# Retrieval gates scattered into a DRAM table by adding indirect DMAs, instead of built by one-hot matmuls

## The chip, the cores and the metric

One core of a Trainium2 chip runs the whole program. The metric is device time in microseconds (us), of which three runs of the kernel before are given. TensorE is called PE in the profile (its weight load PEld), VectorE DVE, ScalarE ACT, GpSimd POOL, SyncE SP.

## The reference, cut to what matters

A layer with attention, a gated delta rule and a product-key retrieval of experts ("peer"), followed by a second layer that the change doesn't touch. There are 256 tokens of width 1024, all in float32. The retrieval, in blocks of 128 tokens:

```python
s1, s2 = scores of each of 8 heads against 128 + 128 sub-keys
v1, i1 = lax.top_k(s1, 16); v2, i2 = lax.top_k(s2, 16)
cand_s = v1[..., :, None] + v2[..., None, :]          # 256 candidates a head
cand_i = i1[..., :, None] * 128 + i2[..., None, :]
top_s, pos = lax.top_k(cand_s, 16)
experts = take_along_axis(cand_i, pos); gates = softmax(top_s)
act = gelu(einsum("thkd,td->thk", expert_down[experts], h))
out = einsum("thk,thkd->td", gates * act, expert_up[experts])
```

Each token thus uses 8 x 16 = 128 of the 128 x 128 experts, and an expert that two heads pick gets the sum of their gates.

## The kernel before

The retrieval is computed densely. All 16384 x 256 activations are computed ("down"), multiplied by a gate that is zero for an expert that isn't picked, and multiplied with all of `expert_up` ("up"). Weights stream from DRAM through a ring of four 1 MB slots (`Stream`, loads issued by SP at L94). Each slot is four units of 128 x 512. Every unit is split in a high part (ACT, `split_hi`, L285) and the rest (DVE, `split_lo`, L290), for three float32r products on PE. There are four buffers for the parts, so ACT splits unit u once PE is done with unit u - 4, and DVE and PE follow.

Down is 256 units in 32 groups of 8, each unit 12 matmuls (L1833). After each group, ACT applies Gelu to the group's 128 x 1024 results (`gelu(c)`, L1876), into a staging tile, and issues a store of it to `act_spill` in DRAM (L1880). Up is 256 units as well, each 6 matmuls of 512 columns (L300). For each 8 units of it, ACT loads 512 KB of activations back (`load_acts`, L1886), DVE multiplies them by the gates (`weights`, L2017), ACT and DVE split the products (L1893, L2022), and PE waits for the split.

The gates are made beside down. DVE does the `routing` between its splits: the top 16 of each score row, the candidates, their top 16, and the look-up of the two sub-key indices by comparing and summing (L1940 to L1998), which must be done six units before group 20 (`GATE0`). ACT takes one exponential (L1908), DVE normalizes, PE transposes the picks (six transposes). Then, in 64 of the units from group 20 on, DVE makes for 4 tokens a one-hot of the first index (L2007) and a gated one-hot of the second (L2010), PE multiplies them (L1819) to a 128 x 128 gate matrix for each token, and ACT copies it into the gates' place in SBUF (L1897). PE, ACT and DVE run this order as it is written; nothing is planned at run time.

Ahead of it stands the delta rule's stage (blocks at L1230 and L1321), in which POOL's first instruction is a small memset (L1241) and ACT's are two exponentials (L1249, L1250) and then two larger ones that wait for DVE (L1252, L1253). SP loads tiles of `w_ada` there (`load_fills`, L441), which PE and DVE sum as filler work (L460, L449), seven tiles deep. POOL's only DMAs in the kernel before are two in the first stage (L702, L706) and the gate row's store and load near the end of up (L479, L484).

Of the kernel before, what the change touches and what calls it, by code (L numbers as in the profile page):

```python
# [16 lines left out]
F32 = mybir.dt.float32  # L17
# [126 lines left out]
def build(nc, A, out):  # L144
    with ExitStack() as ctx:
# [7 lines left out]
        act_spill = nc.dram_tensor("act_spill", (P, P * S), F32, kind="Internal").ap()  # L153
# [1072 lines left out]
        qgT = at(O_X_HI + 512, HD, P)  # L1226
        (s_zero, s_gbias, s_gexp, s_diff, s_dexp, s_beg, s_tk, s_kk, s_L, s_dv) = (sem("dn_" + n) for n in (
            "inverse_cleared", "gate_bias_loaded", "gate_exps", "differences", "decays", "beta_decay",
            "k_transposed", "grams", "lower", "steps"))
        with nc.Block() as block:  # L1230
# [417 lines left out]
        with nc.Block() as block:  # L1648
# [5 lines left out]
            def _(sp):  # L1654
# [5 lines left out]
                sp.wait_ge(s_sp, 16)  # L1660

# [100 lines left out]
        GT = 4  # L1762
        NB4 = S // GT
        GATE0 = 20
        slots = [8 * c + u for c in range(GATE0, 31) for u in (1, 2, 3, 5, 6, 7)][:NB4]
        slot_of = {u: b for b, u in enumerate(slots)}
        one1 = [at(O_ONE + i * GT * P, GT, P) for i in range(2)]
        one2 = [at(O_ONE + 1024 + i * GT * P, GT, P) for i in range(2)]
        staged = at(O_ST, 1024)
        G = at(O_R, P, S)  # L1770
        pick = lambda i, t, n=1: at(O_PICKS + i * S + t, n)
        (s_G, s_st, s_route, s_dv, s_e, s_gn, s_t, s_pt, s_o1, s_o2, s_gm, s_ge) = (sem("experts_" + n) for n in (
            "gelu", "acts_stored", "routed", "steps", "exp", "normed", "picks_transposed", "picksT", "onehot1",
            "onehot2", "gate_product", "gate_out"))
# [16 lines left out]
        with nc.Block() as block:  # L1791
            @block.gpsimd
            def _(pool):
                nc.clear_and_free_semaphores(query_sems)
                store_gate(pool)
                load_gate(pool, gate2)
# [14 lines left out]
            def _(pe):  # L1811
                def gates(b):

                    pe.wait_ge(s_o1, b + 1)
                    pe.wait_ge(s_o2, b + 1)
                    if b >= 4:
                        pe.wait_ge(s_ge, b - 3)
                    for j in range(GT):
                        mm = pe.matmul(ps[:, 4 + b % 4, j * P:(j + 1) * P], one1[b % 2][:, j, :], one2[b % 2][:, j, :],  # L1819
                                       start=True, stop=True)  # L1820
                    mm.then_inc(s_gm, 1)

                for c in range(DG):
                    if c >= 2:
                        pe.wait_ge(s_G, c - 1)
                    for k in range(KT):
# [10 lines left out]
                        if u == KT * GATE0 - 2:  # L1837
                            pe.wait_ge(s_gn, 1)
                            transposes(pe, [(psf[:, 2048 + (i * TT + tt) * P:2048 + (i * TT + tt + 1) * P],
                                             pickT[:, i, tt * P:(tt + 1) * P])  # L1840
                                            for i in range(3) for tt in range(TT)]).then_inc(s_t, 1)
                        if u in slot_of:
                            gates(slot_of[u])
# [9 lines left out]
                pe.wait_ge(s_ge, NB4)  # L1853
# [17 lines left out]
            def _(act):  # L1871
                def gelu(c):
                    act.wait_ge(unit_used, used_value(g0 + KT * c + 7))
                    if c:
                        act.wait_ge(s_st, 16 * c)
                    act.activation(staged, psf[:, c % 2 * 1024:(c % 2 + 1) * 1024], ACT.Gelu).then_inc(s_G, 1)  # L1876

                def store(c):
                    act.wait_ge(s_G, c + 1)
                    act.dma_start(act_spill[:, c * 1024:(c + 1) * 1024], staged).then_inc(s_st, 16)  # L1880

                def load_acts(q):
# [3 lines left out]
                    act.dma_start(got[q % 2], act_spill[:, q * 1024:(q + 1) * 1024]).then_inc(s_rd[q % 2], 16)  # L1886
# [8 lines left out]
                def gate_out(b):  # L1895
                    act.wait_ge(s_gm, b + 1)
                    act.copy(G[:, :, b * GT:(b + 1) * GT],  # L1897
                             ps[:, 4 + b % 4, :].rearrange("p (t i) -> p i t", i=P)).then_inc(s_ge, 1)

                for u in range(KT * DG):  # L1900
# [3 lines left out]
                    if u % 8 == 4 and u > 8:  # L1904
                        store(u // 8 - 1)
                    if u == KT * GATE0 - 5:
                        act.wait_ge(s_route, 1)
                        act.activation(pickT[:, 2, :], pickT[:, 2, :], ACT.Exp).then_inc(s_e, 1)  # L1908
                    if u - 5 in slot_of:
                        gate_out(slot_of[u - 5])  # L1910
# [7 lines left out]
                store(DG - 1)  # L1918
                for i in range(3, 2 * P):
                    split_hi(act, n1 + i // UPC, g1 + i, i % UPC, 0)  # L1920
                    q = i // 8
                    if i == 3:
                        act.wait_ge(s_st, 16 * DG)
                        load_acts(1)
                    if i % 8 == (3 if q else 6) and q + 1 < UG:
                        weights_hi(q + 1)
                    if i % 8 == 7 and q + 2 < UG:
                        load_acts(q + 2)
# [4 lines left out]
            def _(dve):  # L1933
# [26 lines left out]
                def routing():  # L1960

                    yield from top16(score, best, best_at, range(TT * 2 * NH))
                    step(dve.tensor_copy(best_ix, u32(best_at)))
                    yield
                    for tt in range(TT):
                        for hd in range(NH):
                            a = best[:, tt * 16 + 2 * hd, :]
                            b = best[:, tt * 16 + 2 * hd + 1, :]
                            one = dve.tensor_tensor(cand[:, tt * NH + hd, :].rearrange("p (a b) -> p a b", b=TOP), wide(a, TOP),
                                                    b.unsqueeze(1).to_broadcast([P, TOP, TOP]), ALU.add)  # L1970
                            yield
                    step(one)
                    yield from top16(cand, picked, picked_at, range(TT * NH))
                    for tt in range(TT):
                        at_ = u32(at(O_V + 1792 + tt * P, P))

                        step(dve.tensor_scalar(u32(part_u[:, 0, :]), at_, 4, None, ALU.logical_shift_right))
                        step(dve.tensor_scalar(u32(part_u[:, 1, :]), at_, 15, None, ALU.bitwise_and))
                        step(dve.tensor_copy(part_of, u32(part_u)))
                        yield  # L1980
                        eq = at(O_M, P, TOP)
                        for half in range(2):
                            step(dve.tensor_tensor(eq, wide(part_of[:, half, :], TOP),
# [960 lines left out]
```

## Time and profile before

| | |
|---|---|
| three runs, median (lowest to highest) | 1671.28 us (1668.65 to 1673.79) |
| profiled execution, span from first to last instruction | 1673.4 us |
| PE, DVE, ACT, POOL busy, share of the span | 95%, 73%, 54%, 2% |
| DMA moved | 313.85 MB, mean 188 GB/s, in the best of 40 slices 364 GB/s |
| mean granted TensorE clock | 0.979 of full speed |

The profiled execution's own time is its span and what lies around it; the span is 2.1 us above the median of the runs and 0.4 us below the slowest, so that span and run time are taken as one here, with an offset of 2.1 us. In the rows, the busy us of a group are the union of its instructions; matmuls overlap, so that the mean ns of one says nothing of their pace, while their count over a stretch does.

### The profile page before, as it was taken

How to read it: one execution, taken by the hardware profiler on the slowest of the kernel's cores; microseconds unless marked ns; L12 is line 12 of the kernel's file. 1: busy time of each engine (PE TensorE's matmuls, PEld its weight loads, DVE VectorE, ACT ScalarE, POOL GpSimd, SP SyncE). 2: the span in 40 equal slices, each digit the busy share in tenths (PEclk: the TensorE clock that was granted, in tenths of full speed). 3: DMA queues.
4: the chain of work that ended last, by engine and by line, in shares of the span. 5: the costliest groups of instructions: out<-in, count | busy, mean ns of one | idle time of the engine just before them, and what ended most of it. 6: DMA issues, size and time to landing. Idle time of an engine off the chain costs nothing. (4 is left out here: it accounts for less than half of the span.)

```text
span 1673.4 us, 26490 instructions
## 1 busy us (share of the span) xinstructions
PE 1587.1 (95%) x10351; PEld 1426.7 (85%) x10351; DVE 1224.7 (73%) x2475; ACT 906.1 (54%) x1518; POOL 41.7 (2%) x82
## 2 busy tenths in 40 slices
PE   5998888999999999999999999899999898989998
PEld 5877767999999999988888888797888677789997
DVE  5876765889997999867667777657886666654664
ACT  6775455554545555555555555546556646455453
POOL 0023000000000000000000000110000000000000
PEclk9999899999999999999999999999999899999999
DMA  9944343667766555567788767554443122445552
GB/s 327 364 161 128 102 159 125 213 217 235 229 205 213 158 158 151 165 229 248 237 293 289 250 234 245 202 177 151 151 150 128 63 89 101 151 151 177 181 197 101
DMA packets 111665, 313.85 MB, mean 188 GB/s; under 512 B 9441, under 2 KB 10041, under 8 KB 102073
## 3 DMA queue, kind: packets, MB, share of 16 engines
q1 hardware_dynamic: 100008, 276.95, 49.9%
q10 hardware_dynamic: 11040, 33.66, 5.9%
q8 instruction: 82, 1.34, 0.3%
q0 software_dynamic: 496, 1.59, 0.3%
q14 instruction: 39, 0.31, 0.1%
HBM read 293.28 MB, written 18.89 MB: 187 GB/s over the span
## 5 line engine op out<-in xcount | busy, mean ns | idle before, releaser
L300 PE MATMUL ps<-parts,parts 128*128 128x512 f32 (+1 forms) x4992 | 972.4, 357 | 20.1 <-DVE parts L290 18.1
L300 PEld LDWEIGHTS ps<-parts,parts 128*128 128x128 f32 x4992 | 824.3, 191 | 155.9 <-DVE parts L290 19.1
L285 ACT CAST parts<-lead 128x512 fp32r<-128x512 f32 x940 | 579.1, 620 | 619.9 <-PE ps L300 394.1
L290 DVE TENSOR_TENSOR parts<-lead,parts 128x512 fp32r<-128x512 f32 x940 | 641.1, 688 | 328.8 <-ACT parts L285 324.8
L1833 PE MATMUL ps<-parts,parts 128*128 128x256 f32 x3072 | 385.3, 285 | 4.5 <-DVE parts L290 4.5
L1833 PEld LDWEIGHTS ps<-parts,parts 128*128 128x128 f32 x3072 | 372.6, 192 | 5.6 <-DVE parts L290 5.6
L376 PE MATMUL ps<-lead,mem 128*128 128x128 f32 (+2 forms) x292 | 46.5, 323 | 41.0 <-ACT mem L520 23.2
L376 PEld LDWEIGHTS ps<-lead,mem 128*128 128x128 f32 (+2 forms) x292 | 40.9, 162 | 47.5 <-ACT mem L520 24.6
L2010 DVE TENSOR_SCALAR mem<-lead,mem 128x128 f32<-128x128 f32 x256 | 71.1, 341 | 0.0
L1819 PE MATMUL ps<-mem 128*128 128x128 f32 x512 | 67.9, 275 | 0.7 <-DVE mem L2010 0.7
L1819 PEld LDWEIGHTS ps<-mem 128*128 128x128 f32 x512 | 62.8, 192 | 1.2 <-issue 1.1
L2007 DVE TENSOR_SCALAR mem<-lead,mem 128x128 f32<-128x128 f32 x256 | 55.5, 280 | 0.0
L2017 DVE TENSOR_TENSOR mem<-mem 128x1024 f32<-128x1024 f32 x32 | 39.1, 1221 | 7.5 <-DMA mem<-act_spill 7.3
L2022 DVE TENSOR_TENSOR parts<-mem,parts 128x1024 fp32r<-128x1024 f32 x32 | 39.0, 1219 | 0.5 <-ACT parts L1893 0.5
L1897 ACT COPY mem<-ps 128x512 f32<-128x512 f32 x64 | 37.0, 579 | 0.0
L1893 ACT CAST parts<-mem 128x1024 fp32r<-128x1024 f32 x32 | 33.5, 1047 | 5.7 <-DVE mem L2017 5.7
L1876 ACT ACTIVATE mem<-ps 128x1024 f32<-128x1024 f32 x32 | 32.7, 1020 | 0.8 <-PE ps L1833 0.8
L2198 PEld LDWEIGHTS ps<-mem 128*128 128x128 f32 x256 | 29.8, 192 | 0.6
L2198 PE MATMUL ps<-mem 128*128 128x128 f32 x256 | 29.9, 275 | 0.0
L1348 PEld LDWEIGHTS ps<-mem 64*64 64x64 f32 x512 | 18.2, 151 | 6.3 <-POOL mem L1333 4.0
L1348 PE MATMUL ps<-mem 64*64 64x64 f32 x512 | 19.5, 238 | 4.3 <-POOL mem L1333 2.5
L479 POOL DMA_DIRECT2D gate_rows<-mem x1 | 0.6, 577 | 885.9 <-DVE mem L2066 885.9
(348 smaller groups left out, 994.3 us busy)
## 6 DMA issues: line engine op xcount, KB each, us to landing
lead<-in_peer_expert_down SPq DMA_DIRECT2D x64, 1024.0 KB, 5.5
lead<-in_peer_expert_up SPq DMA_DIRECT2D x64, 1024.0 KB, 5.8
lead<-in_w_in SPq DMA_DIRECT2D x50, 1024.0 KB, 5.2
lead<-in_w_ffn_in SPq DMA_DIRECT2D x22, 1024.0 KB, 5.2
act_spill<-mem ACTq DMA_DIRECT2D x32, 512.0 KB, 5.1
mem<-act_spill ACTq DMA_DIRECT2D x32, 512.0 KB, 3.6
mem<-in_w_ada SPq DMA_DIRECT2D x29, 512.0 KB, 6.9
lead<-in_w_ffn_out SPq DMA_DIRECT2D x11, 1024.0 KB, 4.9
```

Source lines behind the costliest of these rows:

```text
L285: act.copy(w_hi[g % BUFFERS], st.words(n, u * UNIT, UNIT)).then_inc(hi_ready, 1)
L290: dve.tensor_tensor(w_lo[g % BUFFERS], st.words(n, u * UNIT, UNIT), w_hi[g % BUFFERS].bitcast(F32), ALU.subtract).then_inc(lo_ready, 1)
L300: mm = pe.matmul(o, lhs[a], rhs[b], start=start and i == 0, stop=stop and i == 2, skip_group_check=True, **kw)
L376: last = pe.transpose(o, i, ident[0:i.shape[0], 0:i.shape[0]])
L1348: mm = pe.matmul(ps[rows, bank, u % 4 * HP:(u % 4 + 1) * HP], left[rows, :], right[rows, :], start=True, stop=True)
L1819: mm = pe.matmul(ps[:, 4 + b % 4, j * P:(j + 1) * P], one1[b % 2][:, j, :], one2[b % 2][:, j, :], start=True, stop=True)
L1833: mm = pe.matmul(ps[:, c % 2 * 2 + m // 2, m % 2 * S:(m % 2 + 1) * S], parts[a][:, ms], (x_hi, x_lo)[b][:, k, :], start=k == 0 and i == 0 ...
L2007: one = dve.tensor_scalar(one1[b % 2][:, j, :], iota, pick(0, b * GT + j), None, ALU.is_equal)
L2010: one = dve.tensor_scalar(one2[b % 2][:, j, :], iota, pick(1, b * GT + j), pick(2, b * GT + j), ALU.is_equal, ALU.mult)
L2017: dve.tensor_tensor(got[q % 2], got[q % 2], at(O_R + q * 1024, 1024), ALU.mult).then_inc(s_pr, 1)
L2022: dve.tensor_tensor(a_lo[q], got[q % 2], a_hi[q].bitcast(F32), ALU.subtract).then_inc(s_al, 1)
L2198: mm = pe.matmul(psf[:, 2048 + u * P:2048 + (u + 1) * P], k, q, start=True, stop=True)
```

## The change

The activations stay in SBUF, in the place that the gates had, and nothing of them goes to DRAM. In their stead a table of the gates, `gate_table` (16 MB, cell = 32768 x first index + 256 x second index + token), lies in DRAM. It is cleared in the delta rule's stage: POOL zeroes a 128 x 1024 tile ahead of its other work, and ACT, once that is done and ahead of its exponentials, issues four DMAs of 4 MB that repeat the tile. SP waits for them at the end of the query stage.

The routing is cut in 8 groups, one for each pair of heads and half of the tokens, each spread over 24 units of down; each ends with the cells' numbers and the exponents in SBUF. ACT takes each group's exponential at the 24th unit, and DVE normalizes it in three steps in the next group's units 1 to 3. POOL then issues 256 indirect DMAs, each of which adds 128 gates (one a token) to 128 cells of the table. They go in batches of 16, by head and, within a head, by token half; a batch waits for its group's gates, and for the batch of the head before of the same token half to have landed, since two heads may pick one cell. Four units ahead of the end of down ACT waits for all 256, and then issues the loads of the table, 512 KB for each 8 units of up. The one-hots, their products, their copies, the transposes and the stores are gone.

```diff
+                pool.memset(blank, 0.0).then_inc(s_blank, 1)
+                pool.wait_ge(s_blank, 1)
                 pool.memset(TI_all[HP:P, :, 0:HP], 0.0).then_inc(s_zero, 1)
...
             def _(act):
+                act.wait_ge(s_blank, 1)
+                for i in range(4):
+                    act.dma_start(gate_table[:, i * 8192:(i + 1) * 8192].rearrange("p (a b) -> p a b", b=1024),
+                                  blank.unsqueeze(1).to_broadcast([P, 8, 1024])).then_inc(s_cleared, 16)
                 act.activation(eg_, gc_, ACT.Exp).then_inc(s_gexp, 1)
...
                 sp.wait_ge(s_sp, 16)
+                sp.wait_ge(s_cleared, 64)
...
+        GU = 24
+        read_by = {20: 1, 21: 5, 22: 7, 23: 7, 24: 8}
+        cells = bass.AP(gate_table.tensor, 0, [[1, P * P * S], [1, 1]])
...
+                for hd in range(NH):
+                    for tt in range(TT):
+                        pool.wait_ge(s_gn, TT * (hd // 2) + tt + 1)
+                        if hd:
+                            pool.wait_ge(s_put[tt], 16 * TOP * hd)
+                        for j in range(TOP):
+                            c = (tt * NH + hd) * TOP + j
+                            pool.indirect_dma_start(
+                                out=cells, out_offset=bass.IndirectOffsetOnAxis(ap=picks[0][:, c:c + 1].bitcast(U32), axis=0),
+                                in_=picks[1][:, c:c + 1], in_offset=None, compute_op=ALU.add).then_inc(s_put[tt], 16)
                 store_gate(pool)
...
-                        if u in slot_of:
-                            gates(slot_of[u])
...
                 def gelu(c):
                     act.wait_ge(unit_used, used_value(g0 + KT * c + 7))
-                    if c:
-                        act.wait_ge(s_st, 16 * c)
-                    act.activation(staged, psf[:, c % 2 * 1024:(c % 2 + 1) * 1024], ACT.Gelu).then_inc(s_G, 1)
+                    if c in read_by:
+                        act.wait_ge(s_route, read_by[c])
+                    act.activation(acts[:, c * 1024:(c + 1) * 1024], psf[:, c % 2 * 1024:(c % 2 + 1) * 1024], ACT.Gelu)\
+                        .then_inc(s_G, 1)
...
+                    if u % GU == GU - 1 and u // GU < GROUPS_R:
+                        r = u // GU
+                        act.wait_ge(s_route, r + 1)
+                        v = picks[1][:, gate_cols(r)]
+                        act.activation(v, v, ACT.Exp).then_inc(s_e, 1)
                     if u == KT * DG - 5:
-                        act.wait_ge(s_gm, NB4)
-                        load_acts(0)
+                        for tt in range(TT):
+                            act.wait_ge(s_put[tt], 16 * TOP * NH)
+                        load_gates(0)
...
                     if i == 3:
-                        act.wait_ge(s_st, 16 * DG)
-                        load_acts(1)
+                        load_gates(1)
...
+                    one = dve.scalar_tensor_tensor(out=full_ix, in0=pair[:, :, 0, :], scalar=float(P * S), in1=low_ix,
+                                                   op0=ALU.mult, op1=ALU.add)
...
                     dve.wait_ge(s_rd[q % 2], 16 * (q // 2 + 1))
+                    dve.wait_ge(s_G, q + 1)
```

## Rows read from the trace of the kernel before

**Rows 1.** The page: busy us, share of the span and instructions of each engine.
```profile
PE 1587.1 (95%) x10351; PEld 1426.7 (85%) x10351; DVE 1224.7 (73%) x2475; ACT 906.1 (54%) x1518; POOL 41.7 (2%) x82
```

**Rows 2.** Table of stretches of down: length, busy us (count), PEclk, DMA share, GB/s.
```profile
292.70:507.00 214.30, 212.11 (x1759) 211.29 (x1760) 199.52 (x596) 108.29 (x167) 0.00 (x0) 1.00 0.68 221
530.00:711.00 181.00, 180.25 (x1537) 179.94 (x1537) 168.47 (x592) 93.17 (x161) 0.00 (x0) 1.00 0.52 161
```

**Rows 3.** The timeline: start us, us, what; begin and end of down.
```profile
292.68 7.58 PE L1833 MATMUL ps<-parts,parts 128*128 128x256 f32 x61 [2.35 <-DVE parts L290]
...
709.05 14.64 PE L1833 MATMUL ps<-parts,parts 128*128 128x256 f32 x120
723.52 8.72 PE L300 MATMUL ps<-parts,parts 128*128 128x512 f32 x36
```

**Rows 4.** Table of one stretch ahead of the gates, L1833 alone: PE, PEld busy.
```profile
331.20:474.50 143.30, 142.70 (x1190) 142.50 (x1189) 1.00 0.71 231
```

**Rows 5.** The page, costliest groups: busy us, mean ns; idle before.
```profile
L1819 PE MATMUL ps<-mem 128*128 128x128 f32 x512 | 67.9, 275 | 0.7 <-DVE mem L2010 0.7
...
L1876 ACT ACTIVATE mem<-ps 128x1024 f32<-128x1024 f32 x32 | 32.7, 1020 | 0.8 <-PE ps L1833 0.8
```

**Rows 6.** DVE's groups of instructions from 292.7 to 507.0 us, the costliest.
```profile
L290 DVE TENSOR_TENSOR parts<-lead,parts 128x512 fp32r<-128x512 f32 x147 | 100.0, 686 | 14.2 <-ACT parts L285 13.2
```

**Rows 7.** The timeline around the one change of ACT's table in down.
```profile
504.80 20.32 PE L1833 MATMUL ps<-parts,parts 128*128 128x256 f32 x168
...
516.64 1.28 ACT L1908 ACT_TABLE_LOAD   x1
...
517.93 0.42 ACT L1908 ACTIVATE mem<-mem 128x256 f32<-128x256 f32 x1
```

**Rows 8.** The timeline from the end of down into up, ACT and DVE.
```profile
712.29 0.33 ACTq L1886 DMA_DIRECT2D mem<-act_spill  x1
...
725.14 0.62 ACT L285 CAST parts<-lead 128x512 fp32r<-128x512 f32 x1 [0.40 <-PE ps L300]
...
727.40 0.33 ACTq L1886 DMA_DIRECT2D mem<-act_spill  x1
...
732.63 1.22 DVE L2017 TENSOR_TENSOR mem<-mem 128x1024 f32<-128x1024 f32 x1 [2.86 <-DMA mem<-act_spill]
...
734.52 13.69 PE L300 MATMUL ps<-parts,parts 128*128 128x512 f32 x52 [2.27 <-DVE parts L290]
```

**Rows 9.** The timeline of the delta rule's stage, where the clearing goes.
```profile
138.93 0.52 POOL L1241 MEMSET mem<- 64x512 f32 x1 [18.89 <-POOLq L1014]
138.95 0.21 ACT L1249 ACTIVATE lead<-lead 128x8 f32<-128x8 f32 x1 [0.27 <-PEq L1014]
...
140.77 4.26 SPq L441 DMA_DIRECT2D mem<-in_w_ada  x3
...
141.75 1.06 ACT L1252 ACTIVATE mem<-mem 128x1024 f32<-128x1024 f32 x1 [2.08 <-DVE mem L1271]
...
153.29 2.08 DVE L449 SCALAR_TENSOR_TENSOR mem<-mem,lead 128x1024 f32<-128x1024 f32 x1
```

**Rows 10.** Lines L971 (POOL's largest memset) and L1880 (ACT's stores), ns min/median/max.
```profile
L971 POOL MEMSET mem<- x2: 737/1014/1292, 109.8 to 1081.3; 128x768 f32 x1, 128x896 f32 x1
...
L1880 ACTq DMA_DIRECT2D act_spill<-mem x32: 326/327/360, 307.5 to 724.8; - x32
...
DMA to landing us min/median/max: 2.6/5.1/8.7
```

**Rows 11.** POOL's DMAs in the timeline, and the landing of the gate row's two.
```profile
49.89 1.83 POOL L706 DMA_DIRECT2D mem<-rel_ext  x2 [6.39 <-DMA rel_ext<-mem]
...
1050.67 0.58 POOL L484 DMA_DIRECT2D lead<-gate_rows  x1 [2.97 <-DMA gate_rows<-mem]
...
DMA to landing us min/median/max: 3.2/5.6/8.0
```

**Rows 12.** A POOL instruction that reads SBUF beside a busy DVE, ns min/median/max.
```profile
L978 POOL TENSOR_SCALAR_AFFINE_SELECT mem<-mem x13: 238/537/966, 110.8 to 1091.3; 128x64 f32<-128x64 f32 x13
```

More of the change, by code:

```diff
@@ L1761, in build, with gate_cols @@
         query_sems = retired()
[L1762 to L1774, printed above, removed]
+        PAIRS = NH // 2
+        GROUPS_R = TT * PAIRS
+        GU = 24
+        picks = [at(O_PICKS, 2 * P), at(O_PICKS + 2 * P, 2 * P)]
+        token = at(O_PICKS + 4 * P, TT)
+        low_ix = at(O_PICKS + 4 * P + 64, 2, TOP)
+        full_ix = at(O_PICKS + 4 * P + 96, 2, TOP)
+        eq = at(O_ONE, 4 * TOP, TOP)
+        part_u = at(O_ONE + 1024, 4, TOP)
+        part_of = at(O_ONE + 1088, 4, TOP)
+        found = at(O_ONE + 1152, 4, TOP)
+        acts = at(O_R, P * S)
+        def gate_cols(r):
+            c = (r % TT * NH + r // TT * 2) * TOP
+            return slice(c, c + 2 * TOP)
+        read_by = {20: 1, 21: 5, 22: 7, 23: 7, 24: 8}
+        cells = bass.AP(gate_table.tensor, 0, [[1, P * P * S], [1, 1]])
+        (s_G, s_tok, s_route, s_dv, s_e, s_gn) = (sem("experts_" + n) for n in (
+            "gelu", "tokens", "routed", "steps", "exp", "gates"))
+        s_put = [sem(f"experts_scattered{tt}") for tt in range(TT)]
         n0, g0 = n_down
@@ L1811, in _ @@
             def _(pe):
[L1812 to L1821, printed above, removed]
                 for c in range(DG):
@@ L1836, in _ @@
                         mm.then_inc(unit_used, 1)
[L1837 to L1841, printed above, removed]
-                        if u in slot_of:
-                            gates(slot_of[u])
                 def half(i, tt):
@@ L1917, in _ @@
                 gelu(DG - 1)
-                store(DG - 1)
                 for i in range(3, 2 * P):
@@ new lines, in gates @@
+                def gates(r):
+                    dve.wait_ge(s_e, r + 1)
+                    v = picks[1][:, gate_cols(r)].rearrange("p (h j) -> p h j", j=TOP)
+                    total, inverse = tiny[:, 2 * r:2 * r + 2], tiny[:, 32 + 2 * r:34 + 2 * r]
+                    one = dve.tensor_reduce(total, v, AX, ALU.add)
+                    yield
+                    step(one)
+                    one = dve.reciprocal(inverse, total)
+                    yield
+                    step(one)
+                    dve.tensor_tensor(v, v, wide(inverse, TOP), ALU.mult).then_inc(s_gn, 1)
@@ L2022, in weights_lo @@
                     dve.tensor_tensor(a_lo[q], got[q % 2], a_hi[q].bitcast(F32), ALU.subtract).then_inc(s_al, 1)
-                route = routing()
                 for u in range(KT * DG):
                     if u == KT * DG - 1:
-                        dve.wait_ge(s_ge, NB4)
                         weights(0)
                     split_lo(dve, n0 + u // UPC, g0 + u, u % UPC, 0)
-                    for _ in range(3 if u % 4 == 3 else 2):
-                        next(route, None)
-                    if u == KT * GATE0 - 6:
-                        for _ in route:
-                            pass
-                    if u == KT * GATE0 - 3:
-                        dve.wait_ge(s_e, 1)
-                        g3 = pickT[:, 2, :].rearrange("p (a j) -> p a j", j=TOP)
-                        step(dve.tensor_reduce(tiny[:, 0:16], g3, AX, ALU.add))
-                        step(dve.reciprocal(tiny[:, 16:32], tiny[:, 0:16]))
-                        dve.tensor_tensor(g3, g3, wide(tiny[:, 16:32], TOP), ALU.mult).then_inc(s_gn, 1)
-                    if u == KT * GATE0 + 1:
-                        dve.wait_ge(s_t, 1)
-                        dve.tensor_copy(at(O_PICKS, 3 * S), psf[:, 2048:2048 + 3 * S]).then_inc(s_pt, 1)
-                        dve.wait_ge(s_pt, 1)
-                    if u - 2 in slot_of:
-                        gated_onehots(slot_of[u - 2])
+                    r, v = divmod(u, GU)
+                    if r < GROUPS_R:
+                        if v == 0:
+                            route = routing(r)
+                        for _ in range(3 if v % 2 else 2):
+                            next(route, None)
+                        if v == GU - 3:
+                            for _ in route:
+                                pass
+                    if 1 <= r <= GROUPS_R:
+                        if v == 1:
+                            gate = gates(r - 1)
+                        if 1 <= v <= 3:
+                            next(gate, None)
                 weights_lo(0)
```

117 lines of the change are left out of this document (53 added, 64 removed).

## The prediction

> **What bounds the kernel now.** I read the page first, then the waits, the table of stretches for down, and the timeline at each edge of the change. On the page [rows 1] PE is busy 95% of the span and POOL 2%: work taken off PE counts, and POOL has room. The stretches [rows 2] show down in two parts. Up to 507 us PE is busy 212.1 of 214.3 us with DVE at 199.5: PE sets the pace, DVE is close behind. From 530 to 711 us, with the gates' work, PE is busy 180.3 of 181.0 us. Down runs from 292.7 to 723.5 us [rows 3], 430.8 us, and PE hardly waits in it. The clock is the full one in all of it (granted 1.00, so 2.4 GHz), so a matmul that goes is time that goes, as long as no one else becomes late.
>
> **Part 1, PE's gate products go.** Without them down's matmuls go at 1190 in 143.3 us [rows 4], 0.1204 us each; the last 120 of down, when the gates are done, take 14.47 us [rows 3], 0.1206 each. Down has 256 units x 12 = 3072 of them: 3072 x 0.1204 = 369.9 us. Down gets shorter by 430.8 - 369.9 = 60.9 us. The gates' own row agrees roughly: 512 products, 67.9 us busy, overlapping with others [rows 5]. DVE's one-hots and ACT's copies go too, and they are worth nothing by themselves, since they lay beside PE.
>
> **Part 2, the routing in 8 groups.** DVE's routing is 199.5 - 100.0 = 99.5 us [rows 2, 6], 12.4 us a group. A group has 24 units, 24 x 1.445 = 34.7 us of PE, in which DVE also splits for 24 x 0.686 = 16.5 us: 28.9 of 34.7 us. In the 18 units where the group's steps really lie it is 12.4 + 12.3 of 26.0 us, 95%, as tight as before (93%), where PE lost 2.2 us in the stretch. More small steps wait for their predecessor now, but the four units of buffers smooth that. I take 0, between -2 (the loss goes) and +2.
>
> **Part 3, ACT's exponentials.** Eight instead of one, and each changes ACT's table there and back: 2 x 1.28 us [rows 7] and a short exponential. ACT has 24 x 0.62 + 3 x 1.02 = 17.9 us of work [rows 5, 8] per group of 34.7 us, so the 3 us fit; around the one change before, PE ran 20.3 us without a break [rows 7]. Cost 0, covered by the units that are split ahead; with no cover it would be 8 x 3 = 24 us. In the group of Gelu, an output in SBUF instead of in the staging tile costs the same, and the store's issue (0.33 us on ACT) goes.
>
> **Part 4, the edge into up.** The second load of activations was issued at 727.40 us, after a wait for the last store; DVE then sat 2.86 us for it and PE 2.27 us [rows 8]. The table's load has no store to wait for and can go when the split that starts at 725.14 is handed over, at 725.8: 1.6 us earlier. -1.6 us. The loads themselves are as large as before.
>
> **Part 5, the clearing.** POOL's 128 x 1024 memset is 1.47 us (896 columns take 1.29, [rows 10]), so that ACT may go at 140.4 instead of 138.95 us [rows 9]. It issues four DMAs at 0.33 us and some 0.1 between them [rows 10]: 142.1. Then its two exponentials: 142.9, and the larger one, which began at 141.75, begins 1.15 us late; DVE and the stage's end wait behind it. +1.2 us; bounds 0 and 3.2 (all of ACT's delay). The data, 16 MB are 46 us at the 364 GB/s of the profile's best slice and 73 us at the 231 of [rows 4], so they last from 141 to somewhere between 187 and 214 us. Beside them SP's tile loads: the first is issued at 140.77 and used at 153.29 [rows 9], 12.5 us later; 512 KB land in about 5 us [rows 10], and at half the rate, 10 us, are still there in time. DMA from ACT and from SP do share: ACT's 512 KB stores land in 2.6 us at best and 5.1 in the median beside SP's stream [rows 10], not after a queue of megabytes. The Trainium skill, "DMA: Bandwidth & Descriptors", section "Queues, rings and completion order", says that each engine takes turns among the queues packet by packet; the landings agree.
>
> **Sum, if POOL keeps up.** -60.9 + 0 + 0 - 1.6 + 1.2 = -61.3 us. The profiled span 1673.4 becomes 1612.1; the run's median lies 2.1 us under the span, so 1671.3 - 61.3 = **1610 us**.
>
> **Part 6, does POOL keep up?** This is the choice on which the sign hangs. Let d be the time from one indirect DMA to the next on POOL. ACT's wait stands where the first load is issued now, 11.2 us before the end of down (712.29 against 723.52, [rows 3, 8]): at 292.7 + 369.9 - 11.2 = 651.4 us. Behind it on ACT are the table's first load, then every split of the rest of down and of up; DVE and PE wait for those, so lateness goes into the time one for one. The last DMAs must also land: POOL's DMA that writes DRAM takes 3.2 us [rows 11], so POOL must be done at 648.2. Gates of group 1 are ready at about 292.7 + 2 x 34.7 + 2 = 364.1, and since head 0's first batch alone can go before that, 240 DMAs remain: d must be under 284.1 / 240 = 1.18 us. After group 7, at 572.3, 48 remain: 1.58 us, looser. Each batch waits for one whose last DMA was issued 16 d before, 14.7 us at d = 0.92, longer than the slowest landing of 8.0 [rows 11]: no cost.
>
> The trace has no indirect DMA. Rows near it: one plain DMA of 128 rows holds POOL for 0.58 us, and one of 128 x 8 short rows of 512 B for 0.92 (two in 1.83, [rows 11]). An address for each of 128 cells is nearer to the second: I take 0.92, hidden with 0.26 us to spare on each. A DMA whose offsets are read from SBUF may also be held up by DVE: the same small POOL instruction takes 0.24, 0.54 and 0.97 us (least, median, most, [rows 12]), 0.3 or 0.73 us more beside a busy DVE. That makes d 1.22 or 1.65. The far bound is one DMA at a time, 3.2 us: 240 x 2.02 = 485 us late.
>
> The Trainium skill has a rule against this change ("SBUF — State Buffer", "Who interferes with whom"): DVE instructions with two SBUF inputs lock POOL's reads out, and copies in a two-port mode its descriptor writing; the spread of rows 12 agrees with the first. Its section "A bandwidth-pool intuition that's wrong (but worth ruling out)" has a POOL DMA go from 0.62 to 3.1 us beside such copies. As an estimate from that page, d = 3.1 would be 240 x 1.92 = 461 us late; down's DVE work is splits, not such copies, so I give it no more than the tail of the third case.
>
> **The cases.**
> - Hidden (chance 0.52): d under 1.18 us, 1610 us, its own range 1604 to 1618 from the bounds of parts 2 and 5. For it: POOL is idle all through down, and the 0.92.
> - POOL late, gain left (0.18): d between 1.18 and 1.44, where 240 (d - 1.18) reaches 61.3. At 1.22 it is 10 us late, 1620 us; in the middle 1640.
> - POOL late, slower than before (0.19): d over 1.44. At 1.65, the largest hold-up of rows 12, 240 x 0.47 = 113 us late: 1723 us. This is the case on the other side; it decides at 1.44 us per DMA, half as much again as the 0.92.
> - The cells choke the DMA engines (0.05). The weights, 67.1 MB in 369.9 us, are 181 GB/s; at 0.52 of the engines for 161 GB/s [rows 2] that is 0.59. What is left, 0.41 x 369.9 x 16 engines over 32768 cells, is 74 ns for each read, addition and write. No row prices one. A 4 KB packet (a store of 8 to an engine lands in 2.6 us, [rows 10]) takes 325 ns at most; at 150 ns a cell the engines would need 218 + 307 us: 155 us over, 1765 us.
> - The clearing holds SP's tiles up (0.06): if they go behind all 16 MB, the one due at 153.3 lands at 187: +34, 1644, if not later us. Against it: the stores' landings.
>
> **Numbers.** A change of 0.3% (5 us) is about what a measurement of this kernel can tell from none. Faster by more: 0.52 + 0.17 of the second case + 0.06 = 0.75. Within: 0.02. Slower: 0.23. The range reaches down to 1604 and up over the two middle cases to the third at d = 1.65, 1725 us; left out are the third beyond it (about 0.09) and most of the fourth. It is wide because cases of both signs carry weight; the likeliest one's own is 1604 to 1618.
>
> **What the profile after would show.** Part 1: L1833's 3072 matmuls in 370 us, and no PE work between them. Part 2: DVE under 90% in down's first 192 units and PE with no idle. Part 3: 16 or so table loads, no PE wait at them. Part 6: the distance between POOL's DMAs, and the end of the last against ACT's first load of the table; if ACT waits there for POOL or the scatter's landing, PE has one long gap just before up. Part 5: ACT's larger exponential 1.2 us later, no DVE or PE wait for a `w_ada` tile. What would make the prediction wrong, first of all, is a d over 1.2 us; next a stream load in down that lands late.

## The result, and the profile after

The changed kernel takes 1845.24 us (1843.36 to 1850.15), the kernel before, on the same chip, 1672.53 (1668.65 to 1674.69): a ratio of 1.104, 95% interval 1.1018 to 1.1062. That is 172.7 us slower, where 61 us faster was forecast. The page of the profile after, against [rows 1], says where to look:

```profile
span 1843.4 us, 25145 instructions
PE 1527.2 (83%) x9833; PEld 1369.1 (74%) x9833; DVE 1116.8 (61%) x2022; ACT 892.6 (48%) x1475; POOL 462.8 (25%) x340
...
PE   6994788999999980000699999998999988989999
...
POOL 1013000178788777878200000002000000000000
PEclk9996899999999995555799999999999989999999
DMA  9939453577777762222577887774444322345553
```

PE has 59.9 us less to do than before, as intended, and a hole of four slices near the middle. POOL is at work up to the end of the hole. A smaller dip stands in the fourth slice, where the table is cleared. The timeline of PE, ACT and POOL around the hole (start us, us):

```profile
653.81 31.12 PE L1853 MATMUL ps<-parts,parts 128*128 128x256 f32 x258
893.92 7.79 PE L1853 MATMUL ps<-parts,parts 128*128 128x256 f32 x48 [208.99 <-DVE parts L290]
...
892.08 0.34 ACTq L1895 DMA_DIRECT2D mem<-gate_table  x1
892.52 2.18 ACT L285 CAST parts<-lead 128x512 fp32r<-128x512 f32 x4 [211.77 <-DMA gate_table<-mem]
...
885.53 1.55 POOL L1823 DMA_INDIRECT gate_table<-mem  x1 [0.30 <-issue]
889.05 1.54 POOL L1823 DMA_INDIRECT gate_table<-mem  x1 [1.97 <-issue]
```

PE names DVE, DVE waited for ACT, and ACT for the cells. ACT's wait is the one ahead of the table's first load; it lasts until the 256th indirect DMA, which leaves POOL at 890.59, has landed, and the load is issued at 892.08, 1.5 us behind it. So the kernel waits for POOL. POOL's group, and its timeline near the first of the pauses ("issue" marks idle time that nothing in the profile ends):

```profile
L1823 POOL DMA_INDIRECT gate_table<-mem x256 | 419.6, 1639 | 150.2 <-issue 111.2 <-DVE mem L2023 39.0
...
359.76 1.72 POOL L1823 DMA_INDIRECT gate_table<-mem  x1 [38.98 <-DVE mem L2023]
...
386.11 1.55 POOL L1823 DMA_INDIRECT gate_table<-mem  x1 [0.30 <-issue]
387.96 1.55 POOL L1823 DMA_INDIRECT gate_table<-mem  x1 [0.30 <-issue]
393.44 1.54 POOL L1823 DMA_INDIRECT gate_table<-mem  x1 [3.92 <-issue]
```

An adding DMA holds POOL for 1.55 us, the next begins 0.30 us later, and the 16th, the 32nd and so on wait 1.8 to 4.1 us. The 151 that are issued while DVE works take up to 2.38 us, 1.70 in the mean; the 105 in the hole take at most 1.57. Over all the mean is 1.64. From 359.76 to 890.59 us it is 2.07 us for each of 256: this is the d of the prediction, which took 0.92 and had 1.18 as the limit of what is hidden.

The second loss stands in the delta rule's stage, against [rows 9]:

```profile
139.00 0.95 POOL L1243 MEMSET mem<- 128x1024 f32 x1 [18.92 <-POOLq L1014]
...
139.99 24.72 ACTq L1255 DMA_DIRECT2D gate_table<-mem  x4
164.75 0.21 ACT L1257 ACTIVATE lead<-lead 128x8 f32<-128x8 f32 x1 [26.00 <-issue]
...
140.97 16.82 SPq L441 DMA_DIRECT2D mem<-in_w_ada  x3
...
173.70 1.97 PE L1356 MATMUL ps<-mem 64*64 64x64 f32 x32 [25.53 <-POOL mem L1341]
```

ACT is held for 24.7 us by the issue of four DMAs. It is not the single issue that costs, as narrower stretches of ACT's timeline show, up to 140.6 us and from 152 us:

```profile
139.99 1.02 ACTq L1255 DMA_DIRECT2D gate_table<-mem  x2
...
151.80 12.91 ACTq L1255 DMA_DIRECT2D gate_table<-mem  x1
```

Two DMAs go out in 1.0 us, the third takes 10.7 us and the fourth 12.9. So everything that waits for ACT's exponentials is late: POOL's mask, its products, and PE by 25.5 us. SP's issue of three tiles takes 16.8 us where it took 4.3. The table of stretches (length, busy us of PE, PEld, DVE, ACT, POOL, PEclk, DMA share, GB/s) closes the account:

```profile
321.80:684.93 363.13, 363.13 (x3024) 362.92 (x3024) 276.59 (x763) 204.04 (x306) 256.86 (x151) 1.00 0.72 183
684.93:893.92 208.99, 0.00 (x0) 0.00 (x1) 0.75 (x2) 1.40 (x3) 162.73 (x105) 0.51 0.22 1
893.92:1250.00 356.08, 356.08 (x1585) 295.70 (x1585) 256.60 (x343) 190.09 (x293) 1.19 (x2) 0.99 0.75 254
```

Down begins at 321.8 us and not at 292.7 [rows 3]: +29.1. Its work takes 3024 matmuls in 363.1 us at the full clock, without a gap, and 48 more behind the hole: 370.7 us without the hole, 60.1 less than 430.8. The hole is +209.0. Up, from its first matmul to the transposes that follow it (901.55 to 1256.43, before 723.52 to 1082.64), takes 354.9 us and not 359.1: -4.2. The sum is 29.1 - 60.1 + 209.0 - 4.2 = +173.8; the spans differ by 170.0, and the 3.8 us between them lie behind up, where they were not followed. In the hole the granted clock is 0.51, the lower level of 1.2 GHz; behind it PE works at 0.99 in the stretch, so the hole costs little beyond its length.

### The profile page after: what moved, and what is told of

It reads as the page before. It is cut to its first block and busy times, and to the rows that moved or that the text cites. A ratio compares the mean times of both kernels' runs of the same rounds, so it can differ in the third digit from the quotient of the medians.

```text
span 1843.4 us, 25145 instructions
## 1 busy us (share of the span) xinstructions
PE 1527.2 (83%) x9833; PEld 1369.1 (74%) x9833; DVE 1116.8 (61%) x2022; ACT 892.6 (48%) x1475; POOL 462.8 (25%) x340
## 5 line engine op out<-in xcount | busy, mean ns | idle before, releaser
L1853 PE MATMUL ps<-parts,parts 128*128 128x256 f32 x3072 | 370.9, 284 | 211.3 <-DVE parts L290 211.3
L1823 POOL DMA_INDIRECT gate_table<-mem x256 | 419.6, 1639 | 150.2 <-issue 111.2
L1356 PE MATMUL ps<-mem 64*64 64x64 f32 x512 | 21.5, 251 | 31.2 <-POOL mem L1341 25.5
L2205 PEld LDWEIGHTS ps<-mem 128*128 128x128 f32 x256 | 29.8, 192 | 0.6
L2205 PE MATMUL ps<-mem 128*128 128x128 f32 x256 | 29.9, 275 | 0.0
L971 POOL MEMSET mem<- 128x768 f32 (+1 forms) x2 | 2.0, 1025 | 75.8 <-PE ps L376 45.7
L787 DVE SCALAR_TENSOR_TENSOR lead<-lead 128x1024 f32<-128x1024 f32 x16 | 18.9, 1218 | 1.1 <-DMA lead<-in_w_ada 1.1
L2701 ACT ACTIVATE mem<-mem 128x2048 f32<-128x2048 f32 x8 | 15.3, 1916 | 5.8 <-DVE mem L2414 5.8
```

The lines of the kernel that those rows point to most:

```text
L1356: mm = pe.matmul(ps[rows, bank, u % 4 * HP:(u % 4 + 1) * HP], left[rows, :], right[rows, :], start=True, stop=True)
L1823: pool.indirect_dma_start(out=cells, out_offset=bass.IndirectOffsetOnAxis(ap=picks[0][:, c:c + 1].bitcast(U32), axis=0), in_=picks[1][:, c ...
L1853: mm = pe.matmul(ps[:, c % 2 * 2 + m // 2, m % 2 * S:(m % 2 + 1) * S], parts[a][:, ms], (x_hi, x_lo)[b][:, k, :], start=k == 0 and i == 0 ...
L2205: mm = pe.matmul(psf[:, 2048 + u * P:2048 + (u + 1) * P], k, q, start=True, stop=True)
```

## Experiments

Two theories are told apart. **POOL's pitch**: the hole is 256 DMAs at 2.07 us, and the rest of the change does what was forecast. **The cells' traffic**: additions to single cells in DRAM slow the weights' stream or land late, whatever POOL does. Beside them stands the clearing, with its own question: what of it costs the 29 us. "Before" was run beside them four times over: medians of 1671.07 to 1673.64 us.

**no_scatter.** POOL's loop over the batches is taken out, so that every gate is zero, and ACT waits for the gates and not for the cells.

```diff
-                        for tt in range(TT):
-                            act.wait_ge(s_put[tt], 16 * TOP * NH)
+                        act.wait_ge(s_gn, GROUPS_R)
```

> The changed kernel with all 256 indirect DMAs left out, so that every gate is zero; all else, the clearing too, is as changed. Theory: the one long wait of 212 us behind the scatter is the whole of the loss in the expert stage. Then the time is 1845 - 212 = 1633 us (1628 to 1640), and down takes 370 us. Rival: the table's loads or the activations in SBUF cost something of their own, then it stays above 1650.

Measured: 1633.84 us, ratio 0.9776 (0.9759 to 0.9793). Without the DMAs the same kernel is faster than before, and of the 211.4 us that separate it from the changed one the hole is 209.0.

**pool_clear, both_out, clear_2k.** Three ways to find what the clearing costs. In the first POOL issues the four DMAs, behind its last product of the stage; the second is that without the scatter; the third leaves them with ACT but cuts their rows from 4 KB to 2.

```diff
-                act.wait_ge(s_blank, 1)
-                for i in range(4):
-                    act.dma_start(gate_table[:, i * 8192:(i + 1) * 8192].rearrange("p (a b) -> p a b", b=1024),
-                                  blank.unsqueeze(1).to_broadcast([P, 8, 1024])).then_inc(s_cleared, 16)
...
                 one.then_inc(s_gz, 1)
+                for i in range(4):
+                    pool.dma_start(gate_table[:, i * 8192:(i + 1) * 8192].rearrange("p (a b) -> p a b", b=1024),
+                                   blank.unsqueeze(1).to_broadcast([P, 8, 1024])).then_inc(s_cleared, 16)
```

and in clear_2k:

```diff
-                    act.dma_start(gate_table[:, i * 8192:(i + 1) * 8192].rearrange("p (a b) -> p a b", b=1024),
-                                  blank.unsqueeze(1).to_broadcast([P, 8, 1024])).then_inc(s_cleared, 16)
+                    act.dma_start(gate_table[:, i * 8192:(i + 1) * 8192].rearrange("p (a b) -> p a b", b=512),
+                                  blank[:, 0:512].unsqueeze(1).to_broadcast([P, 16, 512])).then_inc(s_cleared, 16)
```

> The whole scatter; the four clearing DMAs are issued by POOL, behind its last work in the delta rule's stage, instead of by ACT. Theory: ACT was held for 25 us while it issued them, and the data themselves cost nothing: 1845 - 27 = 1818 us (1814 to 1822). Rival: the 16 MB on the DMA engines delay the tiles and weights wherever they run: 1830 us or more.

> No scatter (all gates zero) and the clearing on POOL. Theory: both losses are gone and what is left is the sum of the prediction, 1607 to 1613 us. Rival: some of the PE time that was taken out doesn't come back: 1620 us or more.

> The changed kernel with the clearing in rows of 2 KB instead of 4 KB: the same bytes from ACT, twice as many rows. Theory of rows: ACT is held until a fixed number of rows is left to be moved, so the hold grows from 25 us towards the time of the data, to 33 us or more. Theory of bytes: the hold stays at 25 us.

Measured: pool_clear 1837.91 us (ratio 1.101, 1.0981 to 1.1038), both_out 1630.59 (0.9758, 0.9741 to 0.9776), clear_2k 1855.61 in one run. The first two missed by 20 us, so both of their rivals had the number. POOL's timeline in pool_clear, then ACT's in clear_2k, show why:

```profile
160.77 2.69 POOL L1346 DMA_DIRECT2D gate_table<-mem  x3
201.98 0.88 POOL L1346 DMA_DIRECT2D gate_table<-mem  x1 [38.53 <-issue]
```

```profile
139.88 40.57 ACTq L1255 DMA_DIRECT2D gate_table<-mem  x4
180.50 0.21 ACT L1257 ACTIVATE lead<-lead 128x8 f32<-128x8 f32 x1 [41.86 <-issue]
```

Three DMAs of 1024 rows go out on POOL in 2.7 us, and the fourth is held for 38.5. The stage ends only when all engines have, so the stage waited: PE sits 20.1 us at its end, 2.4 before. It goes on at 214.65 us, 11.8 after the fourth issue; what fills these was not followed. With twice the rows ACT is held for 40.6 us in place of 24.7, though its first DMA, of 2048 rows, still goes out in 0.39 us. So the rows that are under way count, as if only so many could be outstanding, and not the bytes, which are the same; the limit itself was not measured. That the engine which issues is held was the part of the theory that stood; that POOL in ACT's place would not be held, as the forecast of 1818 supposed, was wrong.

**split_clear, split_clear_no_scatter.** Three of the clearing DMAs on POOL in the delta rule's stage, the fourth in the query stage, where POOL has nothing else to do (the diff is against pool_clear); then that without the scatter. All kernels from here on are built on split_clear.

```diff
                 one.then_inc(s_gz, 1)
-                for i in range(4):
+                for i in range(0, 3):
...
                 nc.clear_and_free_semaphores(first_sems)
+                for i in range(3, 4):
+                    pool.dma_start(gate_table[:, i * 8192:(i + 1) * 8192].rearrange("p (a b) -> p a b", b=1024),
+                                   blank.unsqueeze(1).to_broadcast([P, 8, 1024])).then_inc(s_cleared, 16)
```

> The whole scatter; POOL issues three of the clearing DMAs behind its work in the delta rule's stage and the fourth in the query stage. In the version with all four in the first place POOL was held 38.5 us ahead of the fourth, and the stage's end waited 20 us for POOL. Theory: that hold was all that the clearing cost, the 16 MB beside the weights cost nothing: 1838 - 20 = 1818 us (1812 to 1822). Rival: the data themselves delay the weights, 1830 us or more.

> As before it, with no indirect DMA (all gates zero). Theory: what is left is the prediction's sum, 1672.5 - 61 = 1611 us (1606 to 1615). Rival: 1620 us or more, then something beside the scatter and the clearing's hold costs time.

Measured: 1827.81 us (1.094, 1.0906 to 1.0973) and 1617.97 (0.9674, 0.9646 to 0.9703). Both lie 7 to 10 us above what was expected. PE's timeline in split_clear has the rest of the price:

```profile
170.32 1.98 PE L1355 MATMUL ps<-mem 64*64 64x64 f32 x33 [4.24 <-issue]
...
201.81 3.65 PE L376 MATMUL ps<-lead,mem 128*128 128x128 f32 x16 [7.80 <-PEq L1325]
```

Two waits, 4.2 us inside the stage (1.0 before) and 7.8 at its end (2.4 before), make down begin at 303 us, 10 us later than before. SP's issue of weight tiles is slow meanwhile (three in 11.0 us from 167.44 on); that the waits come from there was not tried by itself.

**half_scatter, three_quarters_scatter.** Heads 0 to 3, and 0 to 5: 128 and 192 DMAs.

```diff
-                for hd in range(NH):
+                for hd in range(4):
...
-                            act.wait_ge(s_put[tt], 16 * TOP * NH)
+                            act.wait_ge(s_put[tt], 16 * TOP * 4)
```

> The split clearing, and only heads 0 to 3 scattered: 128 indirect DMAs (half of the gates left out). At the 2.07 us that one took on average they end 332 + 265 = 597 us into the span, before ACT's wait at 651. Theory: the scatter costs only by being late, so the time is that of the version with none, 1611 us (within 4). Rival: the cells' additions slow the weight stream, or POOL's work slows DVE, by some 20 us or more.

> The split clearing, and heads 0 to 5 scattered: 192 indirect DMAs (a quarter of the gates left out). Theory of lateness one for one: the end is at 332 + 192 x 2.07 + 3 = 732 us, 81 us behind the 651 of ACT's wait: 1611 + 81 = 1692 us (1684 to 1698). Rival: the lateness is taken up in part by work that goes on, 1675 us or less.

Measured: 1615.1 us (0.9659, 0.9631 to 0.9687) and 1704.61 (1.0198, 1.0169 to 1.0228). PE's timeline in half_scatter at the edge into up, and in three_quarters_scatter:

```profile
671.76 258.59 PE L300 MATMUL ps<-parts,parts 128*128 128x512 f32 x1140
```

```profile
749.63 7.26 PE L1855 MATMUL ps<-parts,parts 128*128 128x256 f32 x48 [84.07 <-DVE parts L290]
```

```profile
744.70 1.55 POOL L1825 DMA_INDIRECT gate_table<-mem  x1 [1.90 <-issue]
```

This separates the theories. 128 DMAs, 16384 cells, cost nothing: the time is that without any (1617.97), down takes 368.7 us, and PE has no gap at all into up. Were the traffic the cost, half of it would show. The trace after has the cells' price: their queue, from 360 to 680 us of down,

```profile
q0 software_dynamic: 21265, 0.09, 14.0%
```

has 21265 packets in 14.0% of the time of 16 engines, 34 ns for each. From 192 on each DMA adds (1827.81 - 1704.61) / 64 = 1.93 us, POOL's pitch in the time when DVE stands still (1.55 + 0.30 + 1.9 / 16 = 1.97). Three quarters came out 12 us over the expectation. The gap is 84.1 us where 81 was expected; most of the rest is the base, 1617.97 and not 1611. (The last DMA ended at 746.3 us and not near 729, but ACT's wait, too, began some 10 us later.)

**plain_cells, cells_of_64, extra_waits, plain_cells_of_64.** What the pitch is made of: without the addition, with half of the cells to a DMA, with three more waits (already satisfied) in each batch, and the first two together. The edits of the first three, in this order:

```diff
-                                in_=picks[1][:, c:c + 1], in_offset=None, compute_op=ALU.add).then_inc(s_put[tt], 16)
+                                in_=picks[1][:, c:c + 1], in_offset=None).then_inc(s_put[tt], 16)
...
-                                out=cells, out_offset=bass.IndirectOffsetOnAxis(ap=picks[0][:, c:c + 1].bitcast(U32), axis=0),
-                                in_=picks[1][:, c:c + 1], in_offset=None, compute_op=ALU.add).then_inc(s_put[tt], 16)
+                                out=cells, out_offset=bass.IndirectOffsetOnAxis(ap=picks[0][0:64, c:c + 1].bitcast(U32), axis=0),
+                                in_=picks[1][0:64, c:c + 1], in_offset=None, compute_op=ALU.add).then_inc(s_put[tt], 16)
...
+                            if j and j % 4 == 0:
+                                pool.wait_ge(s_gn, TT * (hd // 2) + tt + 1)
```

> split_clear with the 256 indirect DMAs writing their cells instead of adding them (gates of experts that two heads picked are lost). Theory: GpSimd's 1.55 us is the making of 128 descriptors' worth of work and does not depend on the add: 1.55 us each, time 1828 +- 4. Rival: the add is what costs, a plain cell costs what the plain DMA of L706 did, 0.92 us: the last is issued near 341 + 256 x 1.3 = 674 and the time falls to about 1618.

> split_clear with each of the 256 indirect DMAs carrying the cells of 64 tokens instead of 128 (half the gates are left out). Theory: most of the 1.55 us is paid for each cell: about 0.8 to 1.0 us each, pitch about 1.3 us, time 1620 to 1640. Rival: it is paid for each DMA: 1.4 us or more each, time 1800 or more, and only fewer DMAs would help.

> split_clear with a wait that is already satisfied ahead of every fourth indirect DMA of a batch (three more in each batch of 16). It tells what the pause of 1.9 to 4.1 us in each batch is. Theory A: it is GpSimd's own, once in 16 DMAs, and stands before the 16th, the 32nd and so on, not where the waits are: the pauses stay at 16 in number, pitch 2.07 us, time 1828 +- 5. Theory B: a wait costs it: some 48 x 4 = 192 more waits (three in each of 16 batches are 48) give 48 more pauses of 2.5 us, about +120 us, 1945.

> plain_cells with the cells of 64 tokens to a DMA (half the gates are left out). From 128 to 64 cells an adding DMA fell from 1.55 to 1.42 us; without the add one of 128 took 0.97 us. Theory (a fixed part of each DMA makes most of it, cells cost about 2 ns each and the add about 0.55 us for each DMA, not for each cell): 0.84 to 0.91 us each, GpSimd's last near 666, time 1618 to 1632. Rival (the add costs by the cell, or plain DMAs cost by the cell): well under 0.8 us and 1618, or 0.97 as before and 1665.

Measured, in one run each: 1669.77, 1770.46, 1833.32 and 1656.73 us. POOL's line in the four kernels, in that order (ns least/median/most, first and last start us):

```profile
L1825 POOL DMA_INDIRECT gate_table<-mem x256: 965/992/2038, 342.8 to 714.4; - x128
```

```profile
L1825 POOL DMA_INDIRECT gate_table<-mem x256: 1419/1423/2336, 340.5 to 810.0; - x128
```

```profile
L1827 POOL DMA_INDIRECT gate_table<-mem x256: 1549/1555/2383, 343.0 to 872.6; - x128
```

```profile
L1825 POOL DMA_INDIRECT gate_table<-mem x256: 897/903/1516, 343.6 to 696.9; - x128
```

From the least of each: a plain DMA of 64 cells takes 0.90 us and one of 128 0.97, 1.1 ns a cell; adding ones 1.42 and 1.55, 2.0 ns a cell. The addition costs 0.52 to 0.58 us for each DMA, and the cells little: if each costs the same, 128 of them make 0.14 of the 0.97 us and 0.26 of the 1.55, and the rest is paid once for each DMA. Half the cells save 57 us in all, by the groups' rows 30 us in the DMAs (mean 1.639 to 1.523 us) and 34 in the idle time between them (111.5 to 77.4), since the pauses are gone, less 3.6 us of wait for the second group's gates. For plain_cells neither theory had the time: its durations were the rival's (0.97, not 1.55), but the last DMA was issued at 714.4 us and not near 674. With a mean of 1.115 us and the gap of 0.30 the pitch is 1.42 and not the 1.3 taken, 30 us, and the wait for the second group's gates is 9.8. PE's gap is 50.5 us. plain_cells_of_64 had the expected duration and came 25 us over, with a mean of 1.008 us, a wait of 13.9 us for the second group's gates, and three short pauses; PE's gap there is 32.0 us.

extra_waits settles half of the pauses' question. POOL's timeline in it:

```profile
371.28 1.55 POOL L1827 DMA_INDIRECT gate_table<-mem  x1 [0.30 <-issue]
376.92 1.55 POOL L1827 DMA_INDIRECT gate_table<-mem  x1 [4.08 <-issue]
```

It is the 16th again, 16 pauses as before, and none at the added waits: the pause is not a wait's. In plain_cells and in cells_of_64 there is none, only waits for DVE's gates, but plain_cells_of_64 has three, of 1.3 to 2.3 us, before its 52nd, 100th and 148th. The two kernels below, whose DMAs are adding ones of 128 cells too, have twelve of 1.8 to 6.2 us, before the 16th, 29th, 31st, 46th and so on. So the step of 16 is no fixed rule, and what causes the pauses stays open.

**half_by_products, half_by_products_rows.** Since 128 DMAs are hidden, token half 0 gets its gates by them and half 1 by the one-hot products of before. The table has half the columns and is cleared by two DMAs, and the activations of half 1 go through DRAM. The second kernel lays a loaded tile out as two blocks of 512 words, so that its rows are 2 KB and not 512 B. The one-hot products are 32 blocks of four tokens, in units 201 to 242. The core of it:

```diff
-                hp, tt = divmod(r, TT)
+                tt, hp = divmod(r, PAIRS)
...
+                    act.activation(acts[:, 4 * c:4 * c + 4, 0:P], pre[:, :, 0:P], ACT.Gelu)
+                    act.activation(staged, pre[:, :, P:S], ACT.Gelu).then_inc(s_G, 1)
...
+                        if u in slot_of:
+                            gates(slot_of[u])
...
-                    act.dma_start(got[q % 2], gate_table[:, q * 1024:(q + 1) * 1024]).then_inc(s_rd[q % 2], 16)
+                    for src, n in ((gate_table, 0), (act_spill, 512)):
+                        act.dma_start(got[q % 2][:, n:n + 512], src[:, q * 512:(q + 1) * 512]).then_inc(s_rd[q % 2], 16)
```

> Tokens 0 to 127 get their gates by the adding indirect DMAs (128 of them), tokens 128 to 255 by one-hot products as in the kernel before (32 blocks of four tokens, three transposes); the table has 128 columns a row group and is cleared by two DMAs on GpSimd in the delta rule stage; the activations of tokens 128 to 255 go through DRAM. The result is the reference's. Theory (GpSimd's pitch of 2.07 us is what makes the change slow, and half the DMAs are hidden): down takes 368.7 us as in half_scatter plus 32 blocks at (430.8 - 368.7) / 64 = 0.97 us, 399.7 us; 1615.1 + 31.0 = 1646, less up to 10 us because half the clearing is gone: 1641, between 1634 and 1649, faster than both kernels. Rival 1: each batch of 16 now waits for its own predecessor's landing, 15 us seven times, so the last lands near 727 and ACT waits some 27 us: about 1668. Rival 2: what the change gave came only with all the products gone (VectorE or ScalarE becomes the bound of down with both kinds of work): 1672 or more.

> half_by_products with the tiles got laid out as two blocks of 512 words, tokens 0 to 127 and tokens 128 to 255, so that each of the two loads writes rows of 2 KB and not of 512 bytes (VectorE's product and TensorE's slices follow the layout). The result is the reference's. In half_by_products up's VectorE waited 35.3 us for the loads of act_spill and TensorE 14.8 us behind it. Theory (the short rows made the loads land late): these 14.8 us go, 1659.7 - 15 = 1645, between 1640 and 1650. Rival (two DMAs in place of one, whatever their rows, or ScalarE's second issue): 1655 to 1660.

Measured: 1659.69 us (0.9928, 0.9908 to 0.9947) and 1651.98 (0.9884, 0.9846 to 0.9922). Both compute the whole of the reference and beat both kernels, by 0.7% and 1.2% against before. Down came out as expected, 295.2 to 693.9 us, 398.7 against 399.7. POOL did wait for landings, as the first rival had it, but six times 2.3 to 5.6 us and not seven times 15; its last DMA ended at 663.6 us, ahead of ACT's first load at 682.8, so nothing waited for it. The miss of 19 us lies in up, 374.7 us long where half_scatter has 354.6. The waits of the first, from 694 to 1080 us, then those of the second:

```profile
DVE mem L2096 <- DMA mem<-act_spill: 35.3, 12, 5.5
ACT parts L1943 <- DVE mem L2096: 29.4, 10, 4.9
PE ps L301 <- DVE parts L291: 14.8, 11, 3.4
```

```profile
DVE mem L2096 <- DMA mem<-act_spill: 16.4, 8, 4.0
ACT parts L1941 <- DVE mem L2096: 13.4, 6, 4.8
```

DVE waited for the loads (7.3 us in the whole kernel before), and longer rows took half of that away, 7.7 us of time, half of the 15 expected. That the 16.4 us of waits that are left come from having two loads in place of one, as the rival has it, was not tried by itself.

## Why the prediction was wrong, by its own steps

- **What bounds, and part 1**: right. Down without the hole is 370.7 us for 369.9 forecast, and 368.7 in half_scatter.
- **Parts 2 and 3**: right. PE is busy in 363.13 of 363.13 us of down, with eight groups' routing and their changes of ACT's table.
- **Part 4**: right in sign, 1.6 us forecast; up is 4.2 us shorter. PE's 2.27 us of [rows 8] are gone altogether, since the table's load waits for no store.
- **Part 5** failed: +1.2 us forecast with 3.2 as its bound, measured +29.1 in the begin of down (10 us of it stay with split_clear). The step that failed is "It issues four DMAs at 0.33 us". The first went out in 0.39 us, though it has 1024 rows and that of [rows 10] 128. The third and the fourth held ACT for 10.7 and 12.9. The sum had no term for an engine that is held by the rows it issued before, and no row of before shows more than two DMAs of 1024 rows behind each other (the two of [rows 11], which were not held).
- **Part 6** failed, and decided the sign. The limit, 1.18 us, was sound: ACT's wait began 358.9 us after down's first matmul, where the forecast had 358.7, and 240 x (2.07 - 1.18) = 214 us of lateness is close to the hole's 209. What failed is "I take 0.92", for a d that was 2.07. The terms of the 2.07 us, from the runs: 0.92 as the row gave; 0.05 more for 128 single cells without an addition (0.97); 0.58 for the addition; 0.30 for the gap; 0.09 for DVE (mean 1.639 against 1.55); 0.13 for the pauses (111.2 / 256 - 0.30). The nearest row was good for what it was, a plain DMA. The sum had no term for the addition and none for what lies between two DMAs. The two plain DMAs of [rows 11], 0.89 and 0.95 us in 1.83, follow each other without a gap, so that row could show neither. With the gap alone d would have been 1.22, over the limit: the 0.26 us to spare did not cover the smaller of the two missing terms. The landing, taken at 3.2 us, was 1.5 at most, which changes little.
- **The case "POOL late, slower"** is what happened, by its mechanism and not by its price. It had DVE's hold-up carry d to 1.65 and ended at 1723 us; DVE gave 0.09 us a DMA, 0.15 in the time in which it worked. The d of 2.07 lies between its 1.65 and the far bound of 3.2, and no term stood there. The forecast's own formula with 2.07, and part 5 at 29.1, gives 1610 + 214 + 28 = 1852, against 1845.24.
- **The hidden case's own range**: the bounds of parts 2 and 5 give 1607 to 1614 us, not the 1604 to 1618 named. Neither comes near what was measured.
- **Contention**: the worst adding DMA beside a busy DVE took 2.38 us against 1.55. The Trainium skill's page "SBUF — State Buffer", section "A bandwidth-pool intuition that's wrong (but worth ruling out)", has a POOL DMA slowed to 3.1 us beside DVE's copies. DVE's work here is mostly splits, and no DMA of these runs took so long: the 3.1 was rightly not taken, though by luck it would have named the sign.
- **The cells choke the engines**: fell, at the rate that POOL reached. half_scatter is not slower than no scatter, and in the changed kernel PE has no gap while 151 DMAs go out beside the weights; a packet took 34 ns, where the forecast had 74 to spare for a cell. All 32768 additions within down, as forecast, would have come half as fast again; no run shows that.
- **The clearing holds SP's tiles**: true in part. SP's issue took 16.8 us for three tiles and not 4.3, and the ten `w_ada` tiles of the stage landed in 25.4 us in the median, not 5.0, with ACT's hold beside it; how much of the 29.1 us is SP's was not separated.

## What to carry to other kernels

Price a queue of small DMAs by pitch, not by the duration of one: the gap, the addition and the pauses more than doubled 0.92 us, and 240 of them had to fit into 284 us. When such work is moved to an idle engine, compute the pitch at which it becomes the bound, and move only the share that fits: 128 DMAs were free, 192 cost more than all that the change gave. And add up the rows of the DMAs that an engine issues behind each other between its other work: two DMAs of 1024 rows went out in 1.0 us, four held ACT for 24.7.

## What the runs showed of the hardware

- An indirect DMA on POOL: 0.90 us for 64 cells, 0.97 for 128; with an addition 1.42 and 1.55; 0.30 us between two. Between two plain DMAs of POOL, not indirect, there was no gap (0.89 and 0.95 us in 1.83).
- Adding ones of 128 cells pause for 1.8 to 4.1 us at every 16th in most kernels, at other steps and up to 6.2 us in the half_by_products kernels. A satisfied wait ahead of one brought no pause.
- A single DMA of 1024 or 2048 rows leaves ACT in 0.39 us. Four DMAs of 4 MB behind each other: ACT held 24.7 us with rows of 4 KB, 40.6 us with rows of 2 KB; on POOL three go in 2.7 us and a fourth is held for 38.5.
- 151 adding DMAs, 19328 additions to single cells in DRAM in 325 us beside 183 GB/s, did not hold PE up; 34 ns a packet on an engine.
